# Weighted sums of V as three fp32r products, run two groups behind the scores, in an RWKV-7 and forgetting-attention trunk

## The chip, the cores and the metric

The kernel runs on one core of one Trainium2 chip. The metric is the device time of one execution in microseconds (us), the median of three runs. Five engines work side by side, each through its own queue in program order, and meet at semaphores: TensorE (PE, with its weight loads shown apart as PEld), VectorE (DVE), ScalarE (ACT), GpSimd (POOL) and SyncE (SP), which issues loads.

## The reference, cut to what matters

The model has two layers over 1024 tokens plus 16 meta tokens, with 16 heads of 64 channels. Layer A (a recurrence) takes the first part of the time and is not touched, except for semaphores that are renamed. Layer B is causal attention with forget gates, and the change is in its last step:

```python
def one_block(args):            # 128 queries; the kernel takes 512 at a time
    logits = (einsum('bhqn,bhkn->bhqk', qb, kh) * scale + cqb[..., None] - ck[:, :, None, :])
    logits = where(key_pos[None, :] <= q_pos[:, None], logits, -inf)
    p = softmax(logits, axis=-1)
    return einsum('bhqk,bhkn->bhqn', p.astype(vh.dtype), vh)
```

Everything is float32. A plain float32 matmul is issued as two TensorE instructions, and the names fp32r and high and low half stand for this: a value x is copied to the type fp32r (the high half), and x minus that copy, again as fp32r, is the low half. A product of two such values is then made of three fp32r matmuls: high by high, low by high and high by low.

## The kernel before, in words

Layer B is worked through in eight rounds, p = 0 to 7, of two heads each: the even head (e = 0) and the odd head (e = 1). A head has 14 units. A unit is one tile of 128 keys against one block of up to 512 queries, with 512, 400, 272, 144 and 16 query columns in the first block's five units and 4 x 512, 512, 400, 272, 144 and 16 in the second's nine (4736 columns a head). The units are taken in eight groups, `GROUPS`: (0, 1), (2, 3), (4), (5, 6), (7, 8), (9, 10), (11, 12), (13).

For a group, the step "scores" makes the logits in PSUM, transposed (keys down, queries across), with three fp32r terms packed in two matmuls and a bfloat16 matmul for the causal mask (L2534 to L2538). ScalarE takes the exponential of each unit into one of four buffers `pt` (L1330). The step "weighted" (L2563) multiplies V, with 64 columns of ones beside it so that the row sums come out too, with `pt`, in float32, into one of two PSUM banks. After the last unit of a query block ScalarE and VectorE copy the two halves out (L1343, L1838).

Between the scores and the weighted sums of a group, `order` puts the work of the next heads, from a list by group (`fill`): "proj" projects K, Q, V and Z of the next round with 24 fp32r matmuls for each third of the tokens (L2460 to L2462), and ScalarE copies the result (L1236); "sumsq" is the head norm (L2475; logarithms L1249, root L1273); "vrow" transposes V, and ScalarE copies it out (L1305 to L1309); "stackk" and "stackq" build the high and low halves of K and Q (ScalarE L1289 and L1295, VectorE L1803, L1804 and L1810 to L1812); "smax" computes the logits once ahead to find a maximum for each query (L2506 and L2510), with VectorE reducing each piece (L1822) and only two PSUM banks for it, so that each piece waits for the reduction of the last but one; "split_b" splits weights (high on ScalarE, L1188, low on GpSimd, L879). The last round has no further heads, and its fill is the first products of the output projection (L1877 to L1879).

The order is written out by hand, one list for all engines; each engine walks through it and issues its part of each step, so that a step's place in the list is its place in every queue. The steps of a group in the list are: fill[g], scores g + 1, weighted g.

## Time and profile before

| | us |
|---|---|
| median of 3 runs | 1923.61 (1923.52 to 1925.65) |
| the profiled execution | 1921.38 |
| its span, first to last instruction | 1919.6 |
| TensorE busy | 1836.2 (96%) |
| VectorE busy | 977.6 (51%) |
| ScalarE busy | 946.9 (49%) |
| GpSimd busy | 431.8 (22%) |
| share of TensorE in the chain that ended last | 88% |
| heads of layer B in the trace | about 1134 to 1836 |

A share of time is a mean over stages. The span minus an engine's busy time is its idle time; that of TensorE is what a wait can cost, and that of the others is free until TensorE waits for them. A TensorE record's duration has a fixed part of pipeline in it, so that records overlap: what a matmul costs is the distance from its start to the next start in a stretch without waits. The mean granted TensorE clock is 0.977 of full speed.

### The profile page before, as it was taken

The page shows a single profiled execution, that of the slowest core. Times are in us where ns is not written, and L with a number is a line of the kernel's source. Part 1 is how long each engine was busy: PE and PEld are TensorE (multiplying, and loading weights), DVE is VectorE, ACT ScalarE, POOL GpSimd, SP SyncE. Part 2 cuts the span into 40 slices and gives each one's busy share as a digit, 9 for nine tenths or more (in the row PEclk, how much of TensorE's full clock was granted, in tenths as well). Part 3 has the DMA queues.
Part 4 walks back from the last instruction along what each step waited for, and adds up shares of the span by engine and source line. Part 5 has one row for each costly group of instructions (what it writes and reads, how often), then busy time and mean ns, then how long its engine had stood idle before and what let it go on. Part 6 is the DMA issues. An engine that isn't in the chain of part 4 may idle for free.

```text
span 1919.6 us, 55790 instructions
## 1 busy us (share of the span) xinstructions
PE 1836.2 (96%) x24271; PEld 1596.3 (83%) x24271; DVE 977.6 (51%) x1873; ACT 946.9 (49%) x1712; POOL 431.8 (22%) x425
## 2 busy tenths in 40 slices
PE   6899999999999999999798999999999999999898
PEld 5798989898998989998698778888888888887676
DVE  7456665666666665666433652534344444344521
ACT  6455454545555554544323525364645555555621
POOL 2223142423323242421000321212121213111010
PEclk8999999999999999999799989999999999999899
DMA  6101010100101010101242110111111101111334
GB/s 234 45 11 45 6 52 9 45 16 28 31 19 42 6 52 9 52 9 30 85 147 103 46 34 16 35 29 28 29 28 29 38 24 39 28 29 28 99 100 136
DMA packets 103735, 89.85 MB, mean 47 GB/s; under 512 B 4101, under 2 KB 95864, under 8 KB 103240
## 3 DMA queue, kind: packets, MB, share of 16 engines
q1 hardware_dynamic: 99544, 66.41, 11.9%
q0 software_dynamic: 3168, 17.14, 2.8%
q8 instruction: 194, 3.18, 0.7%
q10 hardware_dynamic: 784, 2.76, 0.4%
q14 instruction: 45, 0.37, 0.1%
HBM read 64.96 MB, written 21.33 MB: 45 GB/s over the span
## 4 chain that ended last, share of the span: by engine, by line
PE 88%; DVE 5%; ACT 3%; issue 2%; DMA 1%; POOL 0%; SPq 0%; DVEq 0%; ACTq 0%; POOLq 0%
PE ps L1951 8%; PE ps L2563 7%; PE ps L1952 6%; PE ps L2460 6%; PE ps L1953 6%; PE ps L2461 6%; PE ps L2462 6%; PE ps L1877 3%; PE ps L2043 3%; PE ps L1879 3%; PE ps L1878 3%; PE ps L2062 3%; PE ps L2534 2%; PE ps L2506 2%; PE ps L2535 2%
## 5 line engine op out<-in xcount | busy, mean ns | idle before, releaser
L1951 PE MATMUL ps<-xh,wh 128*128 128x258 f32 (+1 forms) x1024 | 320.5, 313 | 4.1 <-ACT arena L1045 2.7
L1952 PE MATMUL ps<-xh,wl 128*128 128x258 f32 (+1 forms) x1024 | 291.6, 285 | 0.0
L1953 PE MATMUL ps<-xl,wh 128*128 128x258 f32 (+1 forms) x1024 | 291.1, 284 | 0.0
L2460 PE MATMUL ps<-xh,wh 128*128 128x348 f32 x744 | 254.5, 342 | 3.3 <-ACT arena_b L1305 3.3
L2461 PE MATMUL ps<-xh,wl 128*128 128x348 f32 x744 | 240.1, 323 | 0.0
L2462 PE MATMUL ps<-xl,wh 128*128 128x348 f32 x744 | 239.8, 322 | 0.0
L1822 DVE TENSOR_REDUCE arena_b<-ps 128x1 f32<-128x144 f32 (+4 forms) x224 | 106.2, 506 | 205.6 <-PE ps L2510 171.7
L1951 PEld LDWEIGHTS ps<-xh,wh 128*128 128x128 f32 x1024 | 193.8, 189 | 16.7 <-ACT arena L1045 4.6
L1952 PEld LDWEIGHTS ps<-xh,wl 128*128 128x128 f32 x1024 | 194.5, 190 | 1.9
L1953 PEld LDWEIGHTS ps<-xl,wh 128*128 128x128 f32 x1024 | 193.6, 189 | 0.0
L1014 ACT ACTIVATE arena<-ps,pp 128x257 f32<-128x257 f32 (+1 forms) x128 | 61.3, 479 | 227.2 <-PE ps L1953 227.2
L1236 ACT ACTIVATE arena_b<-ps 128x348 f32<-128x348 f32 x96 | 43.7, 458 | 238.6 <-PE ps L2462 238.5
L2563 PE MATMUL ps<-arena_b 128*128 128x512 f32 (+4 forms) x448 | 160.6, 475 | 0.0
L2460 PEld LDWEIGHTS ps<-xh,wh 128*128 128x128 f32 x744 | 141.6, 190 | 8.6 <-ACT arena_b L1305 4.3
L2461 PEld LDWEIGHTS ps<-xh,wl 128*128 128x128 f32 x744 | 141.0, 190 | 5.7 <-issue 0.3
L2462 PEld LDWEIGHTS ps<-xl,wh 128*128 128x128 f32 x744 | 140.6, 189 | 0.0
L879 POOL TENSOR_TENSOR wl<-wr,wh 128x1024 fp32r<-128x1024 f32 x30 | 73.2, 2441 | 262.1 <-ACT wh L1188 257.6
L1528 DVE SCALAR_TENSOR_TENSOR arena<-ps,pp,arena 128x256 f32<-128x256 f32 (+1 forms) x128 | 62.1, 485 | 123.6 <-ACT arena L1014 123.6
L1330 ACT ACTIVATE arena_b<-ps 128x512 f32<-128x512 f32 (+4 forms) x224 | 90.5, 447 | 64.7 <-PE ps L2538 55.8
L1877 PE MATMUL ps<-xh,wh 128*128 128x348 f32 (+1 forms) x320 | 117.0, 366 | 2.6 <-DVE xl L1509 1.2
L1879 PE MATMUL ps<-xl,wh 128*128 128x348 f32 (+1 forms) x320 | 113.4, 354 | 0.0
L1878 PE MATMUL ps<-xh,wl 128*128 128x348 f32 (+1 forms) x320 | 113.4, 354 | 0.0
(298 smaller groups left out, 4476.6 us busy)
## 6 DMA issues: line engine op xcount, KB each, us to landing
wr<-in_w_in SPq DMA_DIRECT2D x33, 512.0 KB, 4.5
xt_scr<-arena POOLq DMA_DIRECT2D x2, 4176.0 KB, 13.0
wr<-in_kv_w SPq DMA_DIRECT2D x16, 512.0 KB, 4.0
wr<-in_b_w_in SPq DMA_DIRECT2D x16, 512.0 KB, 3.9
arena<-xt_scr SPq DMA_DIRECT2D x8, 522.0 KB, 4.6
arena<-oa_scr SPq DMA_DIRECT2D x8, 520.0 KB, 4.5
wr<-in_w_out SPq DMA_DIRECT2D x8, 512.0 KB, 5.2
ob_scr<-arena_b POOLq DMA_DIRECT2D x16, 256.0 KB, 2.9
```

What stands on the lines that cost most here:

```text
L1330: act.activation(pt[n_ % 4][0:n_k, 0:n_q], ps[0:n_k, B_ST[i], 0:n_q], ACT.Exp, scale=SCALE).then_inc(S.p_exp, 1)
L1822: dve.tensor_reduce(mpart[:, 3 * t + part:3 * t + part + 1], ps[:, B_SM[i % 2], 0:k1 - k0], AX.X, ALU.max).then_inc(S.smax, 1)
L1877: pe.matmul(acc, wh[:, slot, k, 0:width], xh[:, k, t], start=(k == 0), stop=False)
L1878: pe.matmul(acc, wl[:, slot, k, 0:width], xh[:, k, t], start=False, stop=False)
L1879: mm = pe.matmul(acc, wh[:, slot, k, 0:width], xl[:, k, t], start=False, stop=(k == KO - 1))
L1951: pe.matmul(bank, wh[:, j, k, :], xh[:, k, t], start=(k == 0), stop=False)
L1952: pe.matmul(bank, wl[:, j, k, :], xh[:, k, t], start=False, stop=False)
L1953: mm = pe.matmul(bank, wh[:, j, k, :], xl[:, k, t], start=False, stop=(k == KO - 1))
L2460: pe.matmul(bank[:, 0:SEG], wh[:, slot, k, :], xh[:, k, t], start=(k == 0), stop=False)
L2461: pe.matmul(bank[:, 0:SEG], wl[:, slot, k, :], xh[:, k, t], start=False, stop=False)
L2462: mm = pe.matmul(bank[:, 0:SEG], wh[:, slot, k, :], xl[:, k, t], start=False, stop=(k == KO - 1))
L2563: pe.matmul(ps[:, B_PV[qb_], q0 - 512 * qb_:512], vflat[e][0:n_k, kt, :], pt[n_ % 4][0:n_k, 0:n_q], start=(kt == 0), stop=(kt == 4 * qb_ + 4),
```

## The change

V and the exponentials are split into high and low halves. ScalarE's exponential goes to one of two buffers `pt` and, in a new step "high", ScalarE copies it to fp32r; in a new step "low", VectorE subtracts. Four slots of high and low halves lie in weight slots that the heads don't use (`p_store`), and for the last head in K and Q buffers of the other head (`p_last`). V's rows are first copied to `v_rows` (in the buffer `bsq`), then ScalarE makes `vhi` and VectorE `vlo`, with one column block of ones (zeros in `vlo`) between the two heads' V. The weighted sum of a unit is three fp32r matmuls. An exponential waits until the low half of the unit before the last is made (`p_lo`), since it takes that unit's buffer.

The list of steps of a group becomes: scores g, high g, weighted g - 2, up to two leading smax steps of fill[g], low g, the rest of fill[g]; the weighted sums of the last two groups stand at the end of the head. Some semaphores of the forget gate are merged and an unused tile goes.

```diff
-        vflat = [carve_b(NT * P).rearrange("p (t x) -> p t x", t=NT) for _ in range(2)]
-        pt = [carve_b(512) for _ in range(4)]
+        pt = [carve_b(512) for _ in range(2)]
...
+        P_LAG = 2
...
-            steps = [("scores", e, 0)]
+            steps = []
             for g in range(len(GROUPS)):
-                steps += fill[g]
-                if g + 1 < len(GROUPS):
-                    steps += [("scores", e, g + 1)]
-                steps += [("weighted", e, g)]
-            return steps
+                steps += [("scores", e, g), ("high", e, g)]
+                if g >= P_LAG:
+                    steps += [("weighted", e, g - P_LAG)]
+                k = 0
+                while k < min(2, len(fill[g])) and fill[g][k][0] == "smax":
+                    k += 1
+                steps += fill[g][:k] + [("low", e, g)] + fill[g][k:]
+            return steps + [("weighted", e, g) for g in range(len(GROUPS) - P_LAG, len(GROUPS))]
...
                             act.wait_ge(S.st_done, n_ + 1)
+                            if n_ >= 2:
+                                act.wait_ge(S.p_lo, n_ - 1)
+                            act.activation(pt[n_ % 2][0:n_k, 0:n_q], ps[0:n_k, B_ST[i], 0:n_q], ACT.Exp,
+                                           scale=SCALE).then_inc(S.p_exp, 1)
+                    elif kind == "high":
...
+                            act.wait_ge(S.p_exp, n_ + 1)
                             if n_ >= 4:
                                 act.wait_ge(S.pv_done, n_ - 3)
+                            act.activation(p_part(n_, 0)[0:n_k, 0:n_q], pt[n_ % 2][0:n_k, 0:n_q], ACT.Copy)\
+                                .then_inc(S.p_hi, 1)
...
+                            act.wait_ge(S.b_evac, chunk(p, local) + 1)
+                            if p + e > 0:
+                                act.wait_ge(S.pv_done, NU * (2 * p + 1 - e))
+                            act.activation(vhi[:, :, v_cols(e)], rows_v, ACT.Copy).then_inc(S.v_hi, 1)
...
+                        dve.tensor_tensor(vlo[:, :, v_cols(e)], rows_v, f32(vhi[:, :, v_cols(e)]),
+                                          ALU.subtract).then_inc(S.v_lo, 1)
+                    elif kind == "low":
...
+                            dve.wait_ge(S.p_hi, n_ + 1)
+                            dve.tensor_tensor(p_part(n_, 1)[0:n_k, 0:n_q], pt[n_ % 2][0:n_k, 0:n_q],
+                                              f32(p_part(n_, 0)[0:n_k, 0:n_q]), ALU.subtract).then_inc(S.p_lo, 1)
...
-                            pe.matmul(ps[:, B_PV[qb_], q0 - 512 * qb_:512], vflat[e][0:n_k, kt, :],
-                                      pt[n_ % 4][0:n_k, 0:n_q], start=(kt == 0), stop=(kt == 4 * qb_ + 4),
+                            pe.matmul(o, v_h, p_h, start=(kt == 0), stop=False, skip_group_check=True)
+                            pe.matmul(o, v_l, p_h, start=False, stop=False, skip_group_check=True)
+                            pe.wait_ge(S.p_lo, n_ + 1)
+                            pe.matmul(o, v_h, p_l, start=False, stop=(kt == 4 * qb_ + 4),
                                       skip_group_check=True).then_inc(S.pv_done, 1)
```

First place: ScalarE in an odd head, from the exponentials of units 0 and 1 to those of units 2 and 3. Before (L1249 to L1277 are the norm's logarithms, root and the table loads; L1188 the weight split; L1236 the copy of a projection; L1289 is stackk):

```order
L1330 ACTIVATE arena_b<-ps 128x512 [waits pv_done,st_done]
L1330 ACTIVATE arena_b<-ps 128x400 [waits pv_done,st_done]
L1249 ACT_TABLE_LOAD [waits hn_full]
L1249 ACTIVATE arena_b<-ps,cst 128x348 [waits b_done] x3
L1255 ACTIVATE arena_b<-arena_b 64x1024 [waits pv_read]
L1273 ACT_TABLE_LOAD
L1273 ACTIVATE arena_b<-arena_b 128x1044 [waits b_evac]
L1277 ACTIVATE arena_b<-arena_b 64x1024 [waits d_ln]
L1188 ACTIVATE wh<-wr 128x1024 [waits b_done,w_scaled]
L1236 ACTIVATE arena_b<-ps 128x348 [waits b_done]
L1287 DMA kb<-c_scr 2x1044
L1289 ACTIVATE ka<-arena_b 64x1044 [waits hn_full]
```

The same place now, its first rows (L1352 is the exponential, L1362 the high half):

```order
L1352 ACTIVATE arena_b<-ps 128x512 [waits p_lo,st_done]
L1352 ACTIVATE arena_b<-ps 128x400 [waits p_lo,st_done]
L1362 ACTIVATE wh<-arena_b 128x512 [waits pv_done,p_exp]
L1362 ACTIVATE wh<-arena_b 128x400 [waits pv_done,p_exp]
L1269 ACT_TABLE_LOAD [waits hn_full]
L1269 ACTIVATE arena_b<-ps,cst 128x348 [waits b_done] x3
```

The two copies stand ahead of everything that ScalarE does before the exponentials of units 2 and 3.

Second place: VectorE in an odd head, after the norm of Q. Before (L1812 is the last of stackq, L1838 the copy of a finished sum, L1822 the maxima):

```order
L1810 CAST qc<-qa 64x1044 [waits st_hi]
L1811 CAST qa<-qa 64x1044
L1812 TENSOR_TENSOR qb<-arena_b,qa 64x1044
L1838 COPY arena_b<-ps 64x512 [waits pv_done,ob_free]
L1822 TENSOR_REDUCE arena_b<-ps 128x1 [waits smax_done] x8
```

Now (L1837 is the low half of P, for unit 4 and then for units 5 and 6; L1829 the low half of V; L1868 the maxima):

```order
L1856 CAST qc<-qa 64x1044 [waits st_hi]
L1857 CAST qa<-qa 64x1044
L1858 TENSOR_TENSOR qb<-arena_b,qa 64x1044
L1837 TENSOR_TENSOR wl<-arena_b,wh 128x16 [waits p_hi]
L1837 TENSOR_TENSOR wl<-arena_b,wh 128x512 [waits p_hi] x2
L1829 TENSOR_TENSOR vlo<-arena_b,vhi 128x9x64 [waits v_hi]
L1868 TENSOR_REDUCE arena_b<-ps 128x1 [waits smax_done] x4
```

Unit 4's low half stands behind stackq, and the maxima behind two low halves of P and one of V.

Third place: TensorE in an even head, at the scores of units 7 and 8. Before (L2563 is the weighted sum of units 5 and 6, L2475 the norm's sums):

```order
L2534 MATMUL ps<-qa,ka 128x512 [waits p_exp]
L2535 MATMUL ps<-qb,kb 128x512
L2534 MATMUL ps<-qa,ka 128x512
L2535 MATMUL ps<-qb,kb 128x512
L2563 MATMUL ps<-arena_b 128x512 [waits pv_read,pv_free,p_exp]
L2563 MATMUL ps<-arena_b 128x512 [waits p_exp]
L2475 MATMUL ps<-arena_b,head_ones 128x348 [waits smax,hn_sq]
```

Now (L2612 to L2615 are the three products of unit 4):

```order
L2580 MATMUL ps<-qa,ka 128x512 [waits p_exp]
L2581 MATMUL ps<-qb,kb 128x512
L2580 MATMUL ps<-qa,ka 128x512
L2581 MATMUL ps<-qb,kb 128x512
L2612 MATMUL ps<-wh,vhi 128x16 [waits p_hi]
L2613 MATMUL ps<-wh,vlo 128x16
L2615 MATMUL ps<-wl,vhi 128x16 [waits p_lo]
L2521 MATMUL ps<-arena_b,head_ones 128x348 [waits smax,hn_sq]
```

The weighted sums of units 5 and 6 no longer stand between the scores and the norm's sums; the 16 columns of unit 4 do.

## Rows read from the trace of the kernel before

**Rows 1.** Layer B's heads: length, busy us of PE, PEld, DVE, ACT, POOL; clock, DMA, GB/s.
```profile
1134.00:1836.00 702.00, 690.86 (x3866) 564.33 (x3865) 287.40 (x393) 368.92 (x627) 131.64 (x71) 0.99 0.13 34
```

**Rows 2.** Timeline of TensorE (start us, duration us), a weighted sum between fp32r products.
```profile
1809.46 1.75 PE L2563 MATMUL ps<-arena_b 128*128 128x512 f32 x4
1810.74 0.70 PE L1877 MATMUL ps<-xh,wh 128*128 128x512 f32 x1
1811.28 0.39 PE L1878 MATMUL ps<-xh,wl 128*128 128x512 f32 x1
1811.51 0.39 PE L1879 MATMUL ps<-xl,wh 128*128 128x512 f32 x1
```

**Rows 3.** Groups by form (busy us, mean ns), exponential and VectorE's two-input instruction.
```profile
L1330 ACT ACTIVATE arena_b<-ps 128x512 f32<-128x512 f32 x96 | 53.8, 592 | 12.3 <-PE ps L2535 6.8 <-PE ps L2538 3.7
L1849 DVE TENSOR_TENSOR arena_b<-arena_b 64x1024 f32<-64x1024 f32 x15 | 18.3, 1220 | 0.5
```

**Rows 4.** Timeline, ScalarE and TensorE in an odd head.
```profile
1365.70 0.99 ACT L1330 ACTIVATE arena_b<-ps 128x512 f32<-128x512 f32 x2
1371.19 1.75 PE L2563 MATMUL ps<-arena_b 128*128 128x512 f32 x4
1375.87 0.55 ACT L1330 ACTIVATE arena_b<-ps 128x272 f32<-128x272 f32 x2
1376.61 0.17 PE L2534 MATMUL ps<-qa,ka 128*128 128x16 f32 x1
```

**Rows 5.** Timeline, VectorE and ScalarE in the same odd head, later.
```profile
1382.77 1.24 DVE L1812 TENSOR_TENSOR qb<-arena_b,qa 64x1044 fp32r<-64x1044 f32 x1
1383.90 0.55 ACT L1305 ACTIVATE arena_b<-ps 128x448 f32<-128x448 f32 x1
```

**Rows 6.** Waits of TensorE, 1134 to 1836 (us in total, times, longest us).
```profile
PE ps L2506 <- DVE arena_b L1822: 4.9, 3, 2.7
PE ps L2460 <- ACT arena_b L1305: 3.3, 7, 0.5
PE ps L2534 <- ACT arena_b L1330: 1.7, 2, 1.0
```

**Rows 7.** Timeline in an even head: the exponentials of units 2 and 3, and later.
```profile
1413.81 0.58 ACT L1330 ACTIVATE arena_b<-ps 128x272 f32<-128x272 f32 x2
1415.55 2.63 POOL L879 TENSOR_TENSOR wl<-wr,wh 128x1024 fp32r<-128x1024 f32 x1 [2.86 <-ACT wh L1188]
1415.85 3.43 DVE L1812 TENSOR_TENSOR qb<-arena_b,qa 64x1044 fp32r<-64x1044 f32 x1
1417.14 0.17 PE L2534 MATMUL ps<-qa,ka 128*128 128x16 f32 x1
1419.32 0.66 DVE L1822 TENSOR_REDUCE arena_b<-ps 128x1 f32<-128x144 f32 x2
1420.48 0.35 PE L2506 MATMUL ps<-kb,qc 67*128 67x400 f32 x1
```

**Rows 8.** Timeline around an even head's norm.
```profile
1341.69 1.92 PE L2475 MATMUL ps<-arena_b,head_ones 128*128 128x348 f32 x6
1343.08 1.44 ACT L1249 ACTIVATE arena_b<-ps,cst 128x348 f32<-128x348 f32 x3
1345.35 0.29 PE L2506 MATMUL ps<-kb,qc 67*128 67x272 f32 x1
```

**Rows 9.** Timeline of TensorE, two waits between the layers (in brackets).
```profile
1079.75 3.66 PE L2475 MATMUL ps<-arena_b,head_ones 128*128 128x348 f32 x6 [2.89 <-ACT arena_b L1195]
1096.54 1.73 PE L2475 MATMUL ps<-arena_b,head_ones 128*128 128x348 f32 x5 [1.66 <-ACT arena_b L1195]
```

**Rows 10.** Busy time and granted clock after each (columns as in Rows 1).
```profile
1080.00:1083.00 3.00, 3.00 (x7) 1.77 (x7) 1.36 (x3) 2.08 (x3) 0.25 (x1) 0.50 0.06 19
1097.00:1100.00 3.00, 3.00 (x17) 2.49 (x16) 1.23 (x1) 2.95 (x5) 1.04 (x2) 1.00 0.18 28
```

**Rows 11.** Timeline of TensorE in the last round's even head.
```profile
1778.15 0.70 PE L2506 MATMUL ps<-kb,qc 67*128 67x400 f32 x1 [2.69 <-DVE arena_b L1822]
```

More of the change, by code:

```diff
@@ L396, in build, with v_cols, p_part @@
         NU = len(UNITS)
+        v_rows = bsq[:, 0:NT * HD]
+        def v_cols(e):
+            return slice(2 * e * HD, (2 * e + 1) * HD)
+        p_store = [a[:, 2:4, :, :].rearrange("p s k c -> p (s k c)") for a in (wh, wl)]
+        p_last = ((ka[0], qa[0]), (kb2[0], qb2[0]))
+        def p_part(n_, low):
+            i = n_ % 4
+            if n_ // NU == 2 * KO - 1:
+                return p_last[low][i // 2][:, 512 * (i % 2):512 * (i % 2) + 512]
+            return p_store[low][:, 512 * i:512 * i + 512]
         def unit(w):
```

100 lines of the change are left out of this document (56 added, 44 removed).

## The prediction

> **What bounds the kernel now.** I read the page's shares first: TensorE is busy for 96% of the span and makes 88% of the chain that ended last (the small table), so a thing pays or costs only as it moves TensorE. Then the busy times of the heads' stretch [rows 1]: of 702.0 us TensorE is busy for 690.9 at a mean clock of 0.99, ScalarE for 368.9, VectorE for 287.4. The reader is to see two things: 11 us at most are to be had from waits there, and ScalarE and VectorE have 333 and 415 us free, but as a mean over stages. Last I went through the timelines of an odd and an even head, to see how far ahead of TensorE the others are at each handover, because the change gives both of them work and takes TensorE's cover away. This is where the prediction is decided.
>
> **The products.** Before, the weighted sum of 912 columns (units of 512 and 400) starts at 1809.46; L1877 follows, and the next fp32r start after it is at 1811.28, one step of 0.23 us later than L1877's own [rows 2]. So the sum takes 1811.05 - 1809.46 = 1.59 us, 1.74 ns a column. An fp32r product of 512 columns takes that step of 0.23 us, 0.45 ns a column; three take 1.36. The saving is 0.38 ns x 4736 columns = 1.8 us a head, 29 us over 16 heads. That is the whole gain: waits can give back little, since the one that the lag of two groups removes, TensorE for an exponential, is 1.7 us in all in the records [rows 6]; I put 0.4 us for each pair of heads, for shorter gaps that hide in the pipelined ends, between 0 and 1.
>
> **The new work.** A high half is a ScalarE instruction of the shape of the exponential, 0.59 us for 512 columns, and 512 and 400 together take 0.99 [rows 3, 4]. By the first, 1.16 ns a column x 75,776 columns (16 heads) is 88 us of new ScalarE work; V's high halves of 576 columns add some 0.65 x 16 = 10 us. A low half takes as much a column as L1849, 1.22 us for 1024 [rows 3]: 1.19 ns x 75,776 columns = 90 us on VectorE, and 11 for V. On the mean there is room: 333 us free against 98, and 415 against 101. Where nothing waits for them they cost nothing. Merging semaphores, the unused tile and the two fills of ones are outside the chain: nothing either way, 0.5 us at most.
>
> **Where something waits: a pair of heads, place by place.**
>
> (a) Odd head, scores of unit 4. They need the exponentials of units 2 and 3. ScalarE works without a gap from 1365.70 (units 0 and 1) to 1376.42, where those end, and TensorE wants them at 1376.61: 0.2 us ahead [rows 4]. Now ScalarE does the high halves of 0 and 1 first (the first pair of order rows), 0.99 us, less some 0.1 because it starts a little earlier: 1377.3. And TensorE comes sooner: the weighted sum of units 0 and 1, which it did at 1371.19 [rows 4], now stands behind these scores, 1.6 us, so it arrives at 1375.0. The wait is 2.3 us. Bounds: 1.3 (copies half as long, start earlier) and 3.
>
> (b) The same head, the projection of Z behind vrow. It uses the bank that ScalarE empties with L1305, and waits already, 7 times for 3.3 us in all, 0.5 each [rows 6], until 1384.45 [rows 5]. Now unit 4's low half stands behind stackq in VectorE's queue (second pair of order rows), and unit 6's exponential needs its buffer. VectorE's stackq ended at 1384.01 [rows 5]; it comes 0.9 later for ScalarE's copies of (a) and 0.5 for the low halves of 2 and 3, less 0.2 of slack: 1385.2. From there: low half 0.2, exponential 0.6, two high halves 1.06, L1305 0.55, that is 1387.6. TensorE asked at 1383.95; it has 0.6 of sums less before this point and 2.6 of waits more (2.3 of (a), and 0.3 at the scores of units 5 and 6, whose turn hangs on the norm): 1386.0. A wait of 1.6 where there was 0.5; with the 0.3, 1.4 us. Bounds 0 and 3.5.
>
> (c) Even head, scores of unit 4. The exponentials of 2 and 3 end at 1414.39, TensorE asks at 1417.14 [rows 7]; less 1.6 for the moved sum, 1415.5. ScalarE now has 1.0 of high halves and 0.7 of V's high half ahead: 1416.0. Wait 0.5; bounds 0 and 1.
>
> (d) Even head, third piece of the maxima. VectorE's first reduction is at 1419.32 and TensorE wants it done at 1420.48. It started late because L1812 took 3.43 us, not the 1.24 of the other head: GpSimd's L879 ran from 1415.55 to 1418.18, and 1418.18 + 1.1 is where L1812 ended [rows 5, 7]. Now stackq starts 1.6 us later, and then come two low halves (0.5). If the low halves get in before GpSimd, the reduction is done in time; if GpSimd goes first, it is done about 2.1 us late. I take 1.3 (the row shows that GpSimd goes first in this place), bounds 0 and 2.1.
> The Trainium skill has this as a rule (SBUF — State Buffer, "SBUF: two separate sides"): a VectorE instruction with two inputs in SBUF and a GpSimd instruction lock each other out for their whole length, and the first to start wins. The trace agrees, 3.43 us against 1.24. By it every low half is such an instruction, and the upper bound would stand at (d) each time; without it the sum would be 1.1 less for each pair at most, if the wait of the one had come from something else.
>
> (e) Even head, the norm of K. The maxima behind the norm's sums need ScalarE's logarithms, which run at 1343.08 behind the exponentials of units 7 and 8; TensorE asks at 1345.35, after the second of the three ended at about 1344.0: 1.3 ahead [rows 8]. Now two high halves (1.06) and L1343 (0.55) stand before the logarithms, so 1345.7 instead of 1344.0; and the weighted sum of units 5 and 6, 1.7 us up to 1341.69 [rows 8], is gone from TensorE's side (third pair of order rows), so that it asks at 1343.7. Wait 2.0; bounds 1 and 2.7.
>
> A pair of heads therefore loses 2.3 + 1.4 + 0.5 + 1.3 + 2.0 = 7.5 us and gains 2 x 1.8 + 0.4 = 4.0: 3.5 us slower. Seven rounds: 24.5 us. In all other groups a projection of 3.8 us stands between one exponential and its use, and about 1.1 us of copies fit.
>
> The last round has thin fills. Its even head waits already for VectorE, up to 2.69 us [rows 11]; with the sum of units 0 and 1 gone from between, (c) grows there to some 3 to 4 us, and the low halves lie between the reductions. I take 6 us lost against 3.6 gained, +2.4; bounds -2 and +8.
>
> **The sum.** 1921.4 (the profiled execution, 1.8 above its span) + 24.5 + 2.4 = 1948.3. The median of the three runs is 2.2 us above the profiled one: 1950.5, forecast as 1951.
>
> **The rivals.**
> A, the other side: the copies fall in ScalarE's free time. If ScalarE is 2.5 us or more ahead of TensorE at (a) and (e), as 333 us of free time would have it, no wait comes in, and only the products count: 1923.6 - 29 - 3 = 1892 us. It would decide from there on. For it: the means [rows 1]. Against it: leads of 0.2 and 1.3 us at just these places [rows 4, 8], each smaller than the cover that goes. 0.14.
> B: half of it. The odd head's waits come and the even head's don't, as VectorE and ScalarE are 2.8 us ahead at (c): 3.7 lost, 4.0 gained, and the last round between even and 8 slower: 1921 to 1930 us. 0.14.
> C: TensorE's clock falls in the waits. After 2.89 us of idle TensorE the granted clock is 0.50 (1.2 of 2.4 GHz) for three us, after 1.66 us it stays at 1.00 [rows 9, 10]. Waits (a), (b) and (e) lie between. Three us at half rate cost 1.5; once a pair that is 10 us, two or three times a pair 20 to 30: 1961 to 1981 us. For it: (a) and (b) in one head, 8 us apart. Against: a wait split in two by short work, as (e) is. 0.22.
> That the products are not cheaper (fp32r at another pace with V as weights) has no row for it: the scores run the same form. I leave it in the width.
> The forecast has 0.50.
>
> **How the numbers follow.** A change under 0.2%, 3.8 us, is about what a measurement of this kernel can't tell from none. The forecast's own range is 1934 to 1968 by the bounds of (a) to (e), not all at one end. For 8 in 10 I go from 1916, which leaves out A, to 1982. Faster: A and a little of B and of the forecast's low end, 0.17. Same: most of B, which lies around 1923.6, with the rest of it on either side, 0.06. Slower 0.77.
>
> **What would show it.** In the profile after: TensorE's busy time for the three product lines near 103 us plus pipelined ends, where the steps of L2563 come to 132 (1.74 ns x 75,776); waits of TensorE for the exponential (scores of unit 4) of about 2 us seven times in odd heads; waits at the norm's sums or the maxima behind it in even heads for ScalarE; waits of the Z projection for the copy of vrow; TensorE idle of 50 us or more in the heads' stretch instead of 11. A mean clock well under 0.99 there speaks for C. If idle TensorE stays under 15 us, A holds and the prediction is wrong; if the waits are there but for other releasers (weighted sums for a low half), the step on the order of the queues is wrong.

## The result, and the profile after

The changed kernel takes 1988.08 us (median of four runs, 1987.49 to 1989.59) against 1923.61 for the kernel before: a ratio of 1.0333, 95% interval 1.0313 to 1.0353. One of the four runs of the kernel before took 6703 us and is left out of its median. The change is slower, as forecast, but by 64 us where 27 were forecast, and the time lies above the top of the range, 1982. The profiled execution took 1987.49 us, its span 1985.6.

Three pieces of the page of the changed kernel come first, the busy times, the granted clock by slices, and the chain of waits by engine:

```profile
PE 1850.5 (93%) x24495; PEld 1647.6 (83%) x24495; DVE 1131.8 (57%) x2113; ACT 1047.5 (53%) x1952; POOL 431.5 (22%) x424
...
PEclk8999999999999999998998899999999999999799
...
PE 73%; DVE 12%; ACT 9%; issue 4%; DMA 1%; POOL 0%; SPq 0%; ACTq 0%; DVEq 0%; POOLq 0%
```

TensorE's share of the chain fell from 88% to 73%, VectorE's and ScalarE's rose to 12% and 9%. ScalarE is busy for 101 us more and VectorE for 154, both still with over 40% of the span free. The 7 near the end of the clock's row is in the last round; the kernel before has an 8 there. The heads' stretch, with the columns of [rows 1]:

```profile
1138.00:1902.00 764.00, 705.20 (x4086) 617.07 (x4086) 439.21 (x632) 468.62 (x865) 132.87 (x71) 0.95 0.12 32
```

It takes 764 us where [rows 1] has 702, and TensorE is idle for 59 of them, not 11. What it waited for there (us in total, times, longest us; L2580 is the scores, L2552 the maxima, L2506 a projection, L2521 the norm's sums, L2615 the third product), which answers to [rows 6]:

```profile
PE ps L2552 <- DVE arena_b L1868: 16.7, 9, 3.0
PE ps L2580 <- ACT arena_b L1352: 16.2, 10, 4.0
PE ps L2506 <- ACT arena_b L1323: 10.7, 13, 1.8
PE ps L2552 <- ACT arena_b L1269: 7.7, 7, 1.1
PE ps L2521 <- ACT arena_b L1215: 3.3, 7, 0.5
PE ps L2615 <- DVE wl L1837: 1.5, 6, 0.3
```

Hardly any of it is for a low half itself (the last row): at a lag of two groups the sums find their operands ready. It is the work queued behind the copies and the low halves that TensorE waits for.

**Place by place.** The timeline of TensorE in an odd head, the scores of unit 4 (a) and the projection behind vrow (b), where [rows 4, 5] stood, and in the next even head the third piece of the maxima (d) and the norm of K (e), where [rows 7, 8] stood:

```profile
1300.27 0.28 PE L2580 MATMUL ps<-qa,ka 128*128 128x16 f32 x1 [1.58 <-ACT arena_b L1352]
...
1310.63 0.43 PE L2506 MATMUL ps<-xh,wh 128*128 128x348 f32 x1 [1.75 <-ACT arena_b L1323]
...
1348.34 0.45 PE L2552 MATMUL ps<-kb,qc 67*128 67x400 f32 x1 [2.06 <-DVE arena_b L1868]
...
1359.18 2.02 PE L2521 MATMUL ps<-arena_b,head_ones 128*128 128x348 f32 x6 [0.48 <-ACT arena_b L1215]
...
1364.20 0.36 PE L2552 MATMUL ps<-kb,qc 67*128 67x272 f32 x1 [1.10 <-ACT arena_b L1269]
```

These four places are where the prediction put them, with the engines that it named as releasers; (e) is split in two, the norm's sums and the maxima. What VectorE and GpSimd do ahead of (d):

```profile
1343.81 3.45 DVE L1858 TENSOR_TENSOR qb<-arena_b,qa 64x1044 fp32r<-64x1044 f32 x1
1347.29 0.66 DVE L1837 TENSOR_TENSOR wl<-arena_b,wh 128x272 fp32r<-128x272 f32 x2
1347.98 0.65 DVE L1868 TENSOR_REDUCE arena_b<-ps 128x1 f32<-128x144 f32 x2
...
1343.55 2.61 POOL L897 TENSOR_TENSOR wl<-wr,wh 128x1024 fp32r<-128x1024 f32 x1 [4.47 <-ACT wh L1206]
```

L1858 (L1812 of before) runs 3.45 us beside GpSimd's L897, as it did in [rows 7]; the low halves of units 2 and 3 come behind it, and only then the first reduction, which TensorE has been waiting for.

**Group by group.** For the sum I took from each trace the start of the first matmul of each group's scores. The table has the us from one group to the next, in a pair of heads of the middle rounds without a fall of the clock; column 0 is the stretch from the scores of group 0 to those of group 1, column 7 runs to the next head. The kernels between are the experiments below.

| | 0 | 1 | 2 | 3 | 4 | 5 | 6 | 7 | head |
|---|---|---|---|---|---|---|---|---|---|
| odd, before | 6.78 | 6.05 | 4.80 | 7.68 | 7.28 | 5.74 | 2.66 | 4.31 | 45.3 |
| order alone | 6.75 | 5.26 | 5.71 | 7.60 | 5.78 | 5.74 | 3.01 | 5.79 | 45.6 |
| without copies | 6.76 | 5.32 | 5.43 | 7.61 | 5.89 | 5.42 | 2.69 | 5.56 | 44.7 |
| without low halves | 6.76 | 6.27 | 5.43 | 7.89 | 5.91 | 5.42 | 2.51 | 5.55 | 45.7 |
| after | 6.76 | 6.25 | 5.45 | 9.53 | 5.91 | 5.42 | 2.51 | 5.97 | 47.8 |
| even, before | 1.94 | 6.15 | 5.92 | 5.80 | 8.93 | 7.48 | 6.90 | 1.45 | 44.6 |
| order alone | 1.94 | 4.61 | 6.78 | 6.27 | 8.48 | 7.48 | 7.08 | 2.99 | 45.6 |
| without copies | 1.92 | 4.61 | 7.58 | 6.29 | 8.48 | 7.16 | 6.77 | 2.77 | 45.6 |
| without low halves | 1.92 | 5.28 | 6.44 | 6.29 | 9.52 | 7.16 | 6.77 | 2.78 | 46.2 |
| after | 1.92 | 5.28 | 8.70 | 6.29 | 9.52 | 7.16 | 6.77 | 2.77 | 48.4 |

A pair of heads costs 96.2 or 96.3 us instead of 89.9, 6.4 more, and the clock's falls come on top.

**The clock.** Rounds 0 to 6 have no fall of the granted clock before and nine after, 37.5 us at half rate: three behind (a), four behind (d), two behind (b). The busy time and granted clock (columns as in [rows 1]) of three us behind (d) in two even heads, both behind a wait of 2.06 us, and behind (a) in an odd head, a wait of 1.59:

```profile
1446.00:1449.00 3.00, 3.00 (x12) 2.97 (x11) 0.45 (x1) 0.12 (x1) 1.90 (x1) 0.50 0.03 8
1350.00:1353.00 3.00, 3.00 (x21) 2.82 (x20) 0.10 (x2) 1.72 (x4) 1.90 (x1) 1.00 0.00 0
1398.00:1401.00 3.00, 3.00 (x13) 2.99 (x12) 2.81 (x5) 0.13 (x1) 0.00 (x0) 0.53 0.64 180
```

In the first TensorE does 12 matmuls at 1.2 GHz where the second has 21 at 2.4. The same wait is followed by a fall in one round and not in another: 2.06 us with and without, 1.95 with and without, and 1.58 at (a) with and without. What a fall costs depends on its place. Groups 2 and 3 of an even head take 14.99 us without it and 16.6 with a fall of 3.4 us: 1.6 us each. Groups 2 and 3 of an odd head take 14.98 without, and 15.00 with a fall behind (a): nothing, since TensorE comes later to (b) and waits 0.35 us there and not 1.75. The other three of the nine are in the last two of these rounds: one of 3.4 us behind (b) cost 1.4, and two of 6.8 us, behind (b) and behind (d), 2.8 and 3.0. Together the nine cost 12 us.

**The sum.** Seven rounds are 54.6 us longer (42.6 by the pairs and the shorter first head, 12 by the clock), the last even head 8.1, and the part ahead of the first head 3.5: with 0.2 less at the end 66.0, the difference of the spans (1985.6 - 1919.6).

### The profile page after: what moved, and what is told of

Read it like the earlier page. It is cut to its first block, busy times and chain, and to the rows that moved or that the text cites. A ratio compares the mean times of both kernels' runs of the same rounds, so it can differ in the third digit from the quotient of the medians.

```text
span 1985.6 us, 56933 instructions
## 1 busy us (share of the span) xinstructions
PE 1850.5 (93%) x24495; PEld 1647.6 (83%) x24495; DVE 1131.8 (57%) x2113; ACT 1047.5 (53%) x1952; POOL 431.5 (22%) x424
## 4 chain that ended last, share of the span: by engine, by line
PE 73%; DVE 12%; ACT 9%; issue 4%; DMA 1%; POOL 0%; SPq 0%; ACTq 0%; DVEq 0%; POOLq 0%
PE ps L1997 7%; PE ps L1998 6%; PE ps L1999 6%; PE ps L2506 4%; PE ps L2507 4%; PE ps L2508 4%; PE ps L1923 3%; PE ps L2089 3%; PE ps L1925 3%; PE ps L1924 3%; PE ps L2108 3%; DVE wl L1837 3%; PE ps L2552 2%; PE ps L2580 2%; PE ps L2197 2%
## 5 line engine op out<-in xcount | busy, mean ns | idle before, releaser
L2506 PE MATMUL ps<-xh,wh 128*128 128x348 f32 x744 | 257.4, 346 | 10.7 <-ACT arena_b L1323 10.7
L2507 PE MATMUL ps<-xh,wl 128*128 128x348 f32 x744 | 246.3, 331 | 0.0
L2508 PE MATMUL ps<-xl,wh 128*128 128x348 f32 x744 | 245.7, 330 | 0.0
L1997 PEld LDWEIGHTS ps<-xh,wh 128*128 128x128 f32 x1024 | 193.3, 189 | 16.5 <-ACT arena L1063 4.5
L1998 PEld LDWEIGHTS ps<-xh,wl 128*128 128x128 f32 x1024 | 194.0, 189 | 1.9
L1999 PEld LDWEIGHTS ps<-xl,wh 128*128 128x128 f32 x1024 | 193.2, 189 | 0.0
L1868 DVE TENSOR_REDUCE arena_b<-ps 128x1 f32<-128x144 f32 (+4 forms) x224 | 105.8, 505 | 124.4 <-PE ps L2556 92.6
L1837 DVE TENSOR_TENSOR wl<-arena_b,wh 128x512 fp32r<-128x512 f32 (+4 forms) x210 | 136.1, 683 | 65.0 <-ACT wh L1362 63.6
L2506 PEld LDWEIGHTS ps<-xh,wh 128*128 128x128 f32 x744 | 146.7, 197 | 14.6 <-ACT arena_b L1323 12.5
L2507 PEld LDWEIGHTS ps<-xh,wl 128*128 128x128 f32 x744 | 146.1, 196 | 3.7 <-issue 0.2
L2508 PEld LDWEIGHTS ps<-xl,wh 128*128 128x128 f32 x744 | 145.8, 196 | 0.0
L897 POOL TENSOR_TENSOR wl<-wr,wh 128x1024 fp32r<-128x1024 f32 x30 | 74.0, 2465 | 296.3 <-ACT wh L1206 291.0
L1352 ACT ACTIVATE arena_b<-ps 128x512 f32<-128x512 f32 (+4 forms) x224 | 91.8, 447 | 78.0 <-DVE wl L1837 39.5
```

The lines of the kernel that those rows point to most:

```text
L1352: act.activation(pt[n_ % 2][0:n_k, 0:n_q], ps[0:n_k, B_ST[i], 0:n_q], ACT.Exp, scale=SCALE).then_inc(S.p_exp, 1)
L1837: dve.tensor_tensor(p_part(n_, 1)[0:n_k, 0:n_q], pt[n_ % 2][0:n_k, 0:n_q], f32(p_part(n_, 0)[0:n_k, 0:n_q]), ALU.subtract).then_inc(S.p_lo, 1)
L1868: dve.tensor_reduce(mpart[:, 3 * t + part:3 * t + part + 1], ps[:, B_SM[i % 2], 0:k1 - k0], AX.X, ALU.max).then_inc(S.smax, 1)
L1997: pe.matmul(bank, wh[:, j, k, :], xh[:, k, t], start=(k == 0), stop=False)
L1998: pe.matmul(bank, wl[:, j, k, :], xh[:, k, t], start=False, stop=False)
L1999: mm = pe.matmul(bank, wh[:, j, k, :], xl[:, k, t], start=False, stop=(k == KO - 1))
```

## The experiments

Each was run beside the kernel before, whose median was 1924.17, 1923.74 and 1922.79 us in the three batches.

**Lag of one group.**

```diff
-        P_LAG = 2
+        P_LAG = 1
```

> The changed kernel with its weighted sums one group behind the scores and not two. Theory of the cover (the sums moved behind the scores were what TensorE did while ScalarE and VectorE got ready): the waits for the exponential of units 2 and 3, for the maxima and for the norm's sums shrink by the 1.2 to 1.4 us of a moved sum each, the clock falls less often, and the time is about 1945 us (1935 to 1955). Rival, the copies alone fill ScalarE and VectorE: the waits stay and the time is 1980 to 1990.

Measured: 2044.61 us (ratio 1.0627, 1.0609 to 1.0645). The expectation was far off. What TensorE waited for in the heads, then the worst single wait and what stood ahead of it on VectorE and GpSimd:

```profile
PE ps L2615 <- DVE wl L1837: 61.4, 28, 3.5
```

```profile
1476.86 0.39 PE L2615 MATMUL ps<-wl,vhi 128*128 128x272 f32 x1 [3.54 <-DVE wl L1837]
...
1473.05 1.25 DVE L1858 TENSOR_TENSOR qb<-arena_b,qa 64x1044 fp32r<-64x1044 f32 x1
1474.33 2.69 DVE L1837 TENSOR_TENSOR wl<-arena_b,wh 128x272 fp32r<-128x272 f32 x2
...
1473.28 3.22 POOL L897 TENSOR_TENSOR wl<-wr,wh 128x1024 fp32r<-128x1024 f32 x1 [10.22 <-ACT wh L1206]
```

The third product waits for a low half that stands behind all of stackk and stackq in VectorE's queue, and then runs against GpSimd. With the split, the lag of two costs less than a lag of one, though by itself it isn't free, as the next experiment shows. One thing held: (e) is gone at a lag of one (group 4 of the even head 8.91 us against 9.52), since the cover was back.

**The order alone, with the fp32 sums of before.**

```diff
-            steps = [("scores", e, 0)]
+            steps = []
             for g in range(len(GROUPS)):
+                steps += [("scores", e, g)]
+                if g >= 2:
+                    steps += [("weighted", e, g - 2)]
                 steps += fill[g]
-                if g + 1 < len(GROUPS):
-                    steps += [("scores", e, g + 1)]
-                steps += [("weighted", e, g)]
-            return steps
+            return steps + [("weighted", e, g) for g in range(len(GROUPS) - 2, len(GROUPS))]
```

> The kernel before (fp32 sums, no halves) with only the order of steps changed to two groups behind. Cover theory: about 1.4 us of wait at the scores of unit 4 in odd heads, 0.4 at the norm in even heads, some 2 us a round, 1935 to 1942 us. If the copies are the cause and not the order: 1920 to 1926.

Measured: 1939.87 us (1.0073, 1.0055 to 1.0091), as expected: 15.7 us for the order alone. Its trace is 18.5 us longer than that of before, 9.8 of it in rounds 0 to 6. Taking the sum from in front of a handover uncovers waits of TensorE for ScalarE that were hidden: 8.3 us for the exponential in the heads, where [rows 6] has 1.7, of which 0.58 or more at (a) in each odd head; and 0.58 at the norm's sums in each even head. So 0.6 of the 1.58 at (a), and the first part of (e), come with the order and not with the copies.

**No copies on ScalarE, no low halves on VectorE.** The exponential is written to fp32r at once, and the third product uses the high half again; left out is the low half of P, and with it the exponential's wait for it.

```diff
-                            act.activation(pt[n_ % 2][0:n_k, 0:n_q], ps[0:n_k, B_ST[i], 0:n_q], ACT.Exp,
+                            act.activation(p_part(n_, 0)[0:n_k, 0:n_q], ps[0:n_k, B_ST[i], 0:n_q], ACT.Exp,
...
-                            pe.matmul(o, v_h, p_l, start=False, stop=(kt == 4 * qb_ + 4),
+                            pe.matmul(o, v_h, p_h, start=False, stop=(kt == 4 * qb_ + 4),
```

> The changed kernel, but the exponential writes the high half itself, no low half of P is made, and the third product uses the high half again (so the low part of P is left out of the result while TensorE does the same matmuls). Cover theory: only the order's own waits are left, as in the run with the order alone, and the products save 1.35 us a head: 1912 to 1922 us. If three products cost TensorE more than they save: 1940 or more.

Measured: 1935.17 us (1.0052, 1.0034 to 1.0070), only 4.7 below the order alone, where 18 to 28 were expected. TensorE has the same instructions as after, in the same order. The table shows why: two sums of 512 columns give 0.32 us (columns 5 and 6 in either head, as 5.74 to 5.42 and 7.48 to 7.16), the groups with 912 columns 0.2 to 0.3, the small ones nothing, about 1.1 us a head in all. And column 2 of the even head is 0.8 us longer, with a wait of 0.9 at (d); what is new for VectorE there is V's low half. In its trace rounds 0 to 6 are 7.3 us shorter than with the order alone, but the last even head is 3.8 us longer.

**No low halves.** As after, with ScalarE's copies, but without VectorE's low halves of P (left out; the third product uses the high half, and the exponential waits for the copy in place of the low half).

```diff
-                            dve.tensor_tensor(p_part(n_, 1)[0:n_k, 0:n_q], pt[n_ % 2][0:n_k, 0:n_q],
-                                              f32(p_part(n_, 0)[0:n_k, 0:n_q]), ALU.subtract).then_inc(S.p_lo, 1)
```

> The changed kernel without the low halves of P on VectorE (the third product uses the high half again; the low part of P is left out of the result); ScalarE's copies stay. By the queues: the waits for ScalarE at the scores of unit 4 (1.6 us idle) and at the norm (0.5 + 1.1) stay, those for the maxima (2.0) and for the copy of V shrink or go: 1955 to 1968 us. If ScalarE's copies are the whole cause: 1980 or more; if VectorE is: under 1940.

Measured: 1949.38 us (1.0139, 1.0122 to 1.0156), some 6 us below the expected range. By the medians ScalarE's copies cost 14.2 us and VectorE's low halves the remaining 38.7. The waits for the scores and the norm are those of after, and (b) and (d) are gone; TensorE's largest waits in the heads:

```profile
PE ps L2578 <- ACT arena_b L1352: 16.1, 9, 4.0
PE ps L2550 <- ACT arena_b L1269: 7.7, 7, 1.1
PE ps L2504 <- ACT arena_b L1323: 4.3, 13, 0.5
```

So the rest of (a), 1.0 us, and the second part of (e), 1.1, are ScalarE's copies. The wait at (b), 1.75, is 0.23 without VectorE's low halves. At (d) a second thing changed with them, who starts first. VectorE's last step of stackq in an even head, and GpSimd's subtraction beside it:

```profile
1337.75 1.25 DVE L1856 TENSOR_TENSOR qb<-arena_b,qa 64x1044 fp32r<-64x1044 f32 x1
1337.98 3.28 POOL L897 TENSOR_TENSOR wl<-wr,wh 128x1024 fp32r<-128x1024 f32 x1 [4.22 <-ACT wh L1206]
```

Here VectorE is 0.23 us ahead and takes 1.25 us, and GpSimd takes longer; in the changed kernel GpSimd is 0.14 to 0.26 ahead in six even heads, and VectorE takes 3.45. In the kernel without copies GpSimd is ahead too, and (d) is there with 0.8 to 1.1 us although P has no low halves. So a part of the 38.7 us, by column 2 of the even head (7.58 against 6.44) about 1.1 us in each of six heads or 7 us as an estimate, hangs on a start that differs by some tenths of a us.

**GpSimd's subtraction left out.** The low halves of the weights of K, Q, V and Z are not computed in the rounds.

```diff
-                pool.tensor_tensor(wl[:, to, :, :], wr[:, slot, :, :], f32(wh[:, to, :, :]), ALU.subtract)\
-                    .then_inc(S.w_lo, 1)
+                pool.sem_inc(S.w_lo, 1)
```

> The changed kernel without GpSimd's low halves of the weights in the rounds (left out: wl of the K, Q, V and Z weights isn't computed and keeps old values; the products that use it still run). Theory (VectorE's two-input instructions wait for GpSimd's, and the low halves are such): the low halves of P of 144 columns fall from 809 ns to under 450, L1858 in even heads from 3.4 to 1.3 us, the wait (d) of 2 us at the third piece of the maxima goes, and (b) shrinks: 7 x (2.3 + 0.5) = 20 us less and half of the clock's falls, 8: 1960 us, 1950 to 1968. Rival (the low halves are slow for their own sake, or for the order of VectorE's queue): 1984 to 1990 with the durations as they were.

Measured: 1958.38 us (1.0177, 1.0160 to 1.0194): 29.7 us below after, as expected. The groups of VectorE's two-input instructions by form (busy us, mean ns), first after, then without the subtraction, where L1836 and L1857 are after's L1837 and L1858:

```profile
L1837 DVE TENSOR_TENSOR wl<-arena_b,wh 128x512 fp32r<-128x512 f32 x90 | 71.1, 818 | 34.2 <-ACT wh L1362 34.2
L1858 DVE TENSOR_TENSOR qb<-arena_b,qa 64x1044 fp32r<-64x1044 f32 x16 | 33.1, 2068 | 0.2
L1837 DVE TENSOR_TENSOR wl<-arena_b,wh 128x144 fp32r<-128x144 f32 x30 | 24.3, 809 | 0.9
```

```profile
L1836 DVE TENSOR_TENSOR wl<-arena_b,wh 128x512 fp32r<-128x512 f32 x90 | 59.2, 686 | 37.6 <-ACT wh L1361 37.6
L1857 DVE TENSOR_TENSOR qb<-arena_b,qa 64x1044 fp32r<-64x1044 f32 x16 | 19.9, 1243 | 0.2
L1836 DVE TENSOR_TENSOR wl<-arena_b,wh 128x144 fp32r<-128x144 f32 x30 | 19.3, 643 | 1.0
```

The subtraction of GpSimd was what made them long, and with it went (d): column 2 of the even head is 6.44 us again, not 8.70. The low half of 144 columns fell less than I expected (643 ns, not under 450), as GpSimd's multiplication L770 still runs against some of them. In the odd head (b) shrinks, by half. Column 3 doesn't show it, since all seven odd heads of this kernel have a fall of the clock, behind (a) or behind (b). The wait itself, and in the changed kernel what came late:

```profile
1306.81 0.43 PE L2505 MATMUL ps<-xh,wh 128*128 128x348 f32 x1 [0.94 <-ACT arena_b L1322]
```

```profile
1299.80 2.19 DVE L1849 TENSOR_TENSOR ka<-arena_b,ka 64x1044 fp32r<-64x1044 f32 x1 [8.50 <-ACT ka L1309]
```

L1849, the low half of K in stackk, takes 2.19 us beside GpSimd's subtraction and 1.24 without it, and (b) is 0.94 us where it was 1.75. So 0.8 of (b) is GpSimd, and the rest the order of the queue.

**TensorE kept at work in (a) and (d).** Products of no use in the waits of the first seven rounds.

```diff
+                        if e == 1 and g == 2 and p < KO - 1:
+                            for _ in range(10):
+                                pe.matmul(ps[:, B_SM[0], 0:SEG], xh[:, 0, 0:P], xh[:, 0, 0:SEG], start=True, stop=True,
+                                          skip_group_check=True)
```

(and 12 ahead of the third maxima of even heads)

> The changed kernel, with fp32r products of no use put where TensorE waits in the first seven rounds: 10 of 348 columns (1.6 us) ahead of the scores of unit 4 in odd heads, 12 (1.9 us) ahead of the third piece of the maxima in even heads. They fill a wait and lengthen no path if the waits are 1.8 and 2.3 us. Theory (a part of the loss is TensorE's clock, which falls in nine of these waits): the falls after the two places go, and with them some 14 us: 1974 us, 1968 to 1980, mean clock of the heads' stretch 0.98 or more against 0.95. Rival (the falls cost nothing of their own, the waits are the whole loss): 1986 to 1992, or more where a filler outlasts its wait. Second rival: clock falls move to the other waits, 1980 to 1990 at a clock of 0.96 or 0.97.

Measured: 1984.63 us (1.0315, 1.0298 to 1.0332). At (a) and (d) no fall is left, but four odd heads now have one behind (b), where it costs 1.5 us, and two even heads one near their start: six falls and 20.5 us at half rate in the rounds instead of nine and 37.5. The mean clock of the heads is 0.96. The second rival holds: falls move to the next wait, and with three fewer the time is 3.5 us less, a difference that the two intervals don't separate, though the single times do (1983.83 to 1985.54 against 1987.49 to 1989.59). This filler doesn't buy the loss by the clock back.

**A lag that differs by place.**

```diff
-                if g >= P_LAG:
-                    steps += [("weighted", e, g - P_LAG)]
+                steps += [("weighted", e, w) for w in {1: (0,), 3: (1,), 4: (2, 3), 5: (4,), 6: (5,), 7: (6,)}.get(g, ())]
...
-            return steps + [("weighted", e, g) for g in range(len(GROUPS) - P_LAG, len(GROUPS))]
+            return steps + [("weighted", e, 7)]
```

> The changed kernel with a lag that differs by place: the weighted sum of group 0 behind the scores of group 1, of group 1 behind group 3, of 2 and 3 behind group 4, and from there one group behind. That gives TensorE its cover back at the scores of unit 4 (1.6 us, waits (a) and (c)) and at the norm of K (1.7 us, wait (e)), and keeps it where the low halves stand behind stackq. Theory: (a), (c) and (e) lose 4 us a pair, 28 us, and some 10 us of falls of the clock go with them, while (b) and (d) stay: 1950 us, 1942 to 1960. Rival (the sum of group 0 now waits for its own low halves, as the sums did at a lag of one): 1970 to 2000, with waits of L2615's kind for L1837.

Measured: 2022.84 us (1.0539, 1.0496 to 1.0582), a miss of 73 us, above the rival's range too. Column 7 of the odd heads is 10.4 to 10.7 us instead of 5.97: the sum of units 11 and 12 now stands there one group behind its scores and waits for low halves, of which three take 3.85 us on VectorE beside two GpSimd instructions. The timeline of TensorE and VectorE at the end of one odd head:

```profile
1546.96 0.59 PE L2614 MATMUL ps<-wl,vhi 128*128 128x272 f32 x1 [2.25 <-DVE wl L1836]
...
1548.88 0.49 PE L2614 MATMUL ps<-wl,vhi 128*128 128x144 f32 x1 [0.99 <-DVE wl L1836]
...
1545.05 3.85 DVE L1836 TENSOR_TENSOR wl<-arena_b,wh 128x272 fp32r<-128x272 f32 x3
```

**The same, with stackk and stackq a group later.** In even heads both move from fill[0] to the start of fill[1]; in odd heads stackk to the start of fill[1], stackq of fill[2].

> As the kernel with the lag that differs by place, and the copies of stackk and stackq one group later: in even heads both behind the scores of group 1, in odd heads stackk behind the scores of group 1 and stackq of group 2. ScalarE then does the exponentials of units 2 and 3 ahead of them, and VectorE the low halves. Theory: (b) goes (1.4 us a pair) and the rest of (a), 0.7; (d) stays or grows by the later start of the maxima: 10 to 15 us below the same kernel without it, 1937 us, 1925 to 1948. Rival: the maxima start late, the third piece waits for VectorE longer than before, and the norm of Q stands behind: 1955 to 1975, above the other.

Measured: 2003.46 us (1.0402, 1.0360 to 1.0443), 19 below the one before and far above the expectation and its rival, for the same column 7 (10.3 to 11.1 us).

**The changed kernel with only stackk and stackq a group later** (the part for the rounds' odd heads; in even heads both move from fill[0] to fill[1]).

```diff
-                fill[0] = [("sumsq", 1, i) for i in range(3)] + [("den", 0), ("rsq", 1)] + proj(2, 0) + [("stackk", 0)]
-                fill[1] = proj(2, 1) + [("norm", 1), ("stackq", 0)]
-                fill[2] = proj(2, 2)
+                fill[0] = [("sumsq", 1, i) for i in range(3)] + [("den", 0), ("rsq", 1)] + proj(2, 0)
+                fill[1] = [("stackk", 0)] + proj(2, 1) + [("norm", 1)]
+                fill[2] = [("stackq", 0)] + proj(2, 2)
```

> The changed kernel (lag of two everywhere) with the copies of stackk and stackq one group later: in even heads both behind the scores of group 1, in odd heads stackk behind the scores of group 1 and stackq of group 2. Exponentials of units 2 and 3 and the low halves get in ahead of them. Theory (the low halves' and the exponentials' place in the queues makes (a) and (b)): (a) goes, (b) grows by part of it, (d) shrinks by 1: 2.5 us a pair, 17 in all: 1971 us, 1962 to 1980. Rival (what is gained at (a) comes back whole at (b) and (d), since the ring of two scratch tiles and the stack copies are one chain): 1984 to 1992.

Measured: 1977.25 us (1.0272, 1.0244 to 1.0299), as expected: 11 us below after. In odd heads (a) is 0.63 us, what the order alone has, and (b) 0.81 (a head of 45.9 us instead of 47.8); in even heads the maxima now wait for stackq, 0.7 to 0.8, and for VectorE's reduction, 1.7 (49 to 50.8 us). There L1858 no longer meets GpSimd's subtraction. What the places of the queue give here is a fraction of what the work in it costs.

**Two products, order of before.** No low half of P (left out: the weights are rounded to fp32r); high and low half of V.

```diff
-        P_LAG = 2
+        P_LAG = 1
...
                             pe.matmul(o, v_h, p_h, start=(kt == 0), stop=False, skip_group_check=True)
-                            pe.matmul(o, v_l, p_h, start=False, stop=False, skip_group_check=True)
-                            pe.matmul(o, v_h, p_l, start=False, stop=(kt == 4 * qb_ + 4),
+                            pe.matmul(o, v_l, p_h, start=False, stop=(kt == 4 * qb_ + 4),
```

> The order of before (the sum of a group one group behind its scores) with the exponential written straight into fp32r by ScalarE, and two products only, high and low half of V by these weights. Left out: the low half of P, that is, the weights are rounded to fp32r; there is no copy of P on ScalarE and no low half on VectorE. The sum costs 0.90 ns a column instead of 1.74: 4.0 us less a head, some 3.5 after the dearer small units. Theory (the products' saving is real and the new work on ScalarE and VectorE ate it): of 7 us a pair, 0.5 go to (a), whose cover shrinks from 1.6 to 0.9, and about 1.5 to (d), since V's halves remain: 5 us a pair, 35 in the rounds, 2 in the last, less 4 that the lead-in has been later in all kernels with halves of V: 1891 us, 1882 to 1905. Rival (TensorE's time is not what bounds the heads any more once the order is tight): 1910 or more.

Measured: 1900.24 us (0.9880, 0.9858 to 0.9903): 22.6 us faster than before, the fastest version here, inside the expected range and 9 us above its centre. TensorE's share of the chain is back at 81%:

```profile
PE 81%; DVE 9%; ACT 5%; issue 3%; DMA 1%; POOL 0%; SPq 0%; DVEq 0%; ACTq 0%; POOLq 0%
```

It gives up precision that the three products keep. It shows what cheaper arithmetic is worth once neither ScalarE nor VectorE has to split P; it isn't a split of the same precision.

**Two products, two groups behind.**

> The same two products and no low half of P, but with the sums two groups behind. Beside the kernel without copies (1935 us, three products) it drops one product of 0.45 ns x 75,776 columns = 34 us, of which a few come back as waits where the sum was cover: 1904 us, 1897 to 1912. It should be 8 to 15 us behind the same kernel in before's order, because the order of two groups alone cost 15. Rival (order costs nothing once the weights need no copy): within 3 us of the other.

Measured: 1915.92 us (0.9971, 0.9956 to 0.9986), above the expected range, 15.7 behind the other order: the order of two groups costs what it cost in fp32. Beside the kernel without copies the third product is worth 19 us, not the 31 I expected. In its trace, of a run 6 us above the median, the waits for the scores grew, 7.8 to 11.6 us, and one for stackq of 9.4 came in; and there are five falls of the clock in the rounds.

## Why the prediction was right and wrong

Right: the sign, the four large places of the waits with their releasers, and that the copies' engines, free for 40% of the time on the mean, have nothing free where it counts. Rival A (the copies fall in free time) is out, and B (odd heads only) too.

The failed step is the sum for a pair of heads, and with it the clock, which the sum left out: 7.5 us lost against 4.0 gained was 3.5; it is 8.6 lost against 2.2 gained, 6.4, and falls of the clock cost 12 us more. The larger part of what is wrong in the pair lies on the side of the gain.

- **The products.** "The saving is 0.38 ns x 4736 columns = 1.8 us a head, 29 us over 16 heads." The steps of 0.23 us for 512 columns are there, and yet the kernels that differ in the products (order alone, without copies) differ by 0.32 us for 1024 columns and by nothing for units of 144 and 16 columns, 1.1 us a head. The timeline of such a small unit:

```profile
1358.30 0.17 PE L2612 MATMUL ps<-wh,vhi 128*128 128x16 f32 x1
1358.33 0.26 PE L2613 MATMUL ps<-wh,vlo 128*128 128x16 f32 x1
1358.44 0.26 PE L2615 MATMUL ps<-wl,vhi 128*128 128x16 f32 x1
```

  The second product starts 0.03 us after the first, but the third 0.11 later, and the second step of 144 columns is 0.11 too. A sum of 512 columns that follows the bf16 product of the causal mask has a first step of 0.32 us, not 0.23 (1367.96 to 1368.28); behind another sum it is 0.23. I scaled the longest sum by columns. Over seven pairs this is 9.8 us; the 0.4 us of give-back didn't show either, another 2.8.

```profile
1367.96 0.48 PE L2612 MATMUL ps<-wh,vhi 128*128 128x512 f32 x1
1368.28 0.40 PE L2613 MATMUL ps<-wh,vlo 128*128 128x512 f32 x1
1368.52 0.39 PE L2615 MATMUL ps<-wl,vhi 128*128 128x512 f32 x1
```

- **(a)** forecast 2.3, recorded 1.58. **(b)** forecast 1.4 more, recorded 1.75 where there was 0.5. **(c)** forecast 0.5; the scores don't wait, but vrow does a little earlier, 0.45. **(e)** forecast 2.0, recorded 0.48 and 1.10. The forecast's waits run from start to start, so that some 0.25 us belong to each recorded one, as shown below.
- **(d)** forecast 1.3 between 0 and 2.1, recorded 2.06. GpSimd did go first in all six even heads in which the two met, and L1858 took its 3.4 us. The experiment without GpSimd's subtraction shows what hangs on it: 29.7 us, the falls behind (d) among them. It is the upper bound that my own row asked for; I shaded it. In the kernel without low halves VectorE went first, and there was no wait.
  The Trainium skill (SBUF — State Buffer, "SBUF: two separate sides") has the rule that a VectorE instruction with two inputs in SBUF and a GpSimd instruction that reads SBUF lock each other out, and the first to start keeps its pace. The runs agree: L1858 takes 2068 ns on the mean with GpSimd's subtraction and 1243 without; and where VectorE started first, it was GpSimd that took longer, 3.28 us and not 2.6.
- **The low halves** were priced at 90 us by the float32 instruction of [rows 3]; they take 136.1 us in the first 15 heads alone (the mean of 210 is 683 ns). By their lengths without GpSimd beside them (684 ns for 512 columns, where the row gave 610, and 301 for 144) all 16 heads would take 113 us, an estimate; the rest is collisions, which make 13 of the 512-column ones 1664 ns long and seven of the 144-column ones 2483, as medians.
- **The waits as a whole** add up to 7.6 or 7.7 us a pair by their records, 7.1 more than before, and each costs some 0.25 us beyond its record. Around (d), and the same piece without a wait:

```profile
1345.96 0.32 PE L2508 MATMUL ps<-xl,wh 128*128 128x348 f32 x1
1348.34 0.45 PE L2552 MATMUL ps<-kb,qc 67*128 67x400 f32 x1 [2.06 <-DVE arena_b L1868]
1348.64 0.23 PE L2556 MATMUL ps<-causal,identb 128*128 128x128 bf16 x1
```

```profile
1312.65 0.35 PE L2552 MATMUL ps<-kb,qc 67*128 67x400 f32 x1
1312.84 0.23 PE L2556 MATMUL ps<-causal,identb 128*128 128x128 bf16 x1
```

  L2508's record lasts 0.32 us, but its step is 0.16, so 0.16 us are lost before the record of the wait begins; and the first step behind the wait is 0.30 us where it is 0.19 without one. A pair has seven recorded waits and before had one: 1.7 us of this against 0.3. So 7.1 + 1.4 = 8.5 us more of waits, less the 2.2 of the products, make 6.3 of the 6.4 that a pair is longer. With the order alone a pair is 1.4 us longer, 0.7 in records and 0.2 in this way; the other 0.5 stay open.
- **Rival C** got 0.22 and came true on top of the forecast: nine falls, 12 us. I priced it at 1.5 us each, which is right for a fall of 3.4 us behind (d) or (b); of the five in odd heads, where I placed it, the three behind (a) are absorbed by (b). It shouldn't have been a rival but a term. Their number was a matter of luck: the same waits had a fall in some rounds and none in others, and no run here shows what decides it.
- **The last round**: forecast +2.4, measured 8.1 in its even head. The waits there are (c) at 4.00 us and one of 2.97 at the maxima, and the clock is at half for 27.3 us of it instead of 10.2.

```profile
1833.41 0.38 PE L2580 MATMUL ps<-qa,ka 128*128 128x16 f32 x1 [4.00 <-ACT arena_b L1352]
...
1856.10 0.79 PE L2552 MATMUL ps<-kb,qc 67*128 67x512 f32 x1 [2.97 <-DVE arena_b L1868]
```

- **The lead-in**: 3.5 us ahead of the first head, for which I had no term. 2.8 of it come between 1113 and 1123 us, at the first maxima of layer B:

```profile
1114.73 0.61 PE L2552 MATMUL ps<-kb,qc 67*128 67x400 f32 x1 [1.84 <-DVE arena_b L1868]
...
1113.70 0.76 DVE L1829 TENSOR_TENSOR vlo<-arena_b,vhi 128x576 fp32r<-128x576 f32 x1 [0.86 <-ACT vhi L1332]
```

  V's low half, new here, stands ahead of the reduction, and TensorE waits 1.84 us where it waited 0.23; the clock's fall behind it lasts 6.8 us and not 3.4. All kernels here with halves of V have this wait, 1.84 or 1.85 us, and the one with the order alone has 0.25. The other 0.7 come from before that place, where layer A's steps are unchanged. The other kernels reach it 2 to 6.4 us late, the one with the order alone 5.0; no run here shows the cause, and single traces can be compared no closer than that.

Together, for the 39 us between the forecast's 1948.3 and the profiled 1987.5: products and give-back, 4.0 a pair forecast and 2.2 measured, 12.6; time lost a pair, 7.5 forecast and 8.6 measured (6.4 longer in spite of 2.2 saved), 7.7; the clock 12; the last round 5.7; the lead-in 3.5; less 2.2 for the first head and the last boundary, which lose less than the others, and 0.2 at the end: 39.1.

The medians split the loss in another way: order alone +15.7, products and V's halves -4.7, ScalarE's copies +14.2, VectorE's low halves +38.7, with the change of who starts first at (d) and its falls of the clock among them. The last two are what the split of P costs, 53 us for a gain of some 17 on TensorE (1.1 us in each of 16 heads).

## What to carry to other kernels

Moving work from the engine that bounds to engines that are half idle pays only if they are ahead at each handover; go through the handovers one by one, and then add the clock of TensorE and the collisions of VectorE with GpSimd as terms, not as rivals. Price a cheaper matmul by units of each size and by what the whole group gets shorter, not by the step of the largest: here the saving was 60% of that. Where a cheaper form needs splitting of a fresh result, first run it without the splits and see what the idea is worth at most.

## What the runs showed of the hardware

- VectorE's subtraction of 64x1044 takes 3.45 us where GpSimd's subtraction had started 0.14 to 0.26 us before it, and 1.24 alone. Where VectorE had started 0.23 us before, it took 1.25, and GpSimd's took 3.28 instead of 2.6. A pair of low halves of 144 and 272 columns took 2.69 us beside GpSimd's subtraction and 0.66 alone.
- In a sum of three fp32r products, the step from the second to the third is 0.11 us both at 16 and at 144 columns, 0.13 at 272 and 0.23 at 512.
- A wait of TensorE costs some 0.25 us beyond its record: 0.16 by the end of the record before it, and 0.1 by a longer first step (0.30 us, not 0.19).
- After waits of 1.58, 1.95 and 2.06 us the granted clock fell to 0.50 (1.2 GHz) in some rounds, for 3.4 or 6.8 us, and stayed at 1.00 in others. With two of the waits filled, falls came behind others.
- A fall of 3.4 us behind (a) cost nothing, as TensorE then waited less at (b); behind (b) or (d), in front of work without long waits, it cost 1.4 to 1.6 us.
